# Inputs repacked and transposed, the modulations as fused row sums on VectorE, and the opening stage reordered, in a two-layer Hyena / Mamba-2 backbone

## The reference, cut to what matters

```python
sc, scc = silu(c), silu(c_ctx)                  # vectors of 1024
for i in range(2):
    mod  = (sc  @ ada_w[i] + ada_b[i]).reshape(-1, 1, 9, 1024)   # ada_w[i]: 1024 x 9216
    modc = (scc @ ada_w[i] + ada_b[i]).reshape(1, 1, 9, 1024)
    h  = h  + 0.5 * mod[:, :, 2]  * swiglu(adaln(h,  mod, 0),  ffn_in[i, 0], ffn_out[i, 0])
    hc = hc + 0.5 * modc[:, :, 2] * swiglu(adaln(hc, modc, 0), ffn_in[i, 0], ffn_out[i, 0])
    y, yc = mixer(adaln(h, mod, 3), adaln(hc, modc, 3))
    h = h + mod[:, :, 5] * y                    # hc likewise while it is needed
    ...                                         # second FFN, with mod 6, 7, 8
return rms_norm(h) * final_norm_w
# adaln(x, mod, k) = rms_norm(x) * (1 + mod[k + 1]) + mod[k]
```

## Time and profile before

| what | us |
|---|---|
| runs shown | 2270.53, 2270.56, 2274.07 (median 2270.56) |
| profiled execution, its own time | 2273.82 |
| its span, first to last instruction | 2272.0 |
| PE busy | 2100.8 (92% of the span) |
| DVE busy | 1486.2 (65%) |
| ACT busy | 716.9 (32%) |
| POOL busy | 223.8 (10%) |
| DMA | 292.82 MB, mean 129 GB/s |

### The profile page before, as it was taken

The page is one execution under the profiler, slowest core; times in us unless marked ns, Lnnn a source line. Parts: engine busy times, 40 slices in busy tenths (PEclk is TensorE's granted clock), DMA queues, the critical chain, the costliest instruction groups (busy, mean ns, idle before and its releaser), DMA issues.

```text
span 2272.0 us, 25887 instructions
## 1 busy us (share of the span) xinstructions
PE 2100.8 (92%) x10317; PEld 1736.6 (76%) x10317; DVE 1486.2 (65%) x2027; ACT 716.9 (32%) x920; POOL 223.8 (10%) x172
## 2 busy tenths in 40 slices
PE   5999999999978889999999999999999778888998
PEld 2578888878867768888887888887777764478997
DVE  4576666788965667665777666577775558855544
ACT  2432222232310232222324222222444324444443
POOL 1000000100022410000110000011000005540001
PEclk7999999999998989999999999999999889989999
DMA  7344435544410125442654444354332402334554
GB/s 277 130 131 147 148 105 145 176 130 128 159 66 1 56 93 162 143 139 81 177 162 151 143 146 142 110 163 153 111 112 84 148 25 74 93 111 155 181 167 129
DMA packets 288353, 292.82 MB, mean 129 GB/s; under 512 B 8967, under 2 KB 248496, under 8 KB 286256
## 3 DMA queue, kind: packets, MB, share of 16 engines
q1 hardware_dynamic: 284440, 280.26, 39.1%
q10 hardware_dynamic: 3800, 10.98, 1.2%
HBM read 284.86 MB, written 6.36 MB: 128 GB/s over the span
## 4 chain that ended last, share of the span: by engine, by line
PE 74%; DVE 13%; issue 4%; ACT 3%; DMA 3%; POOL 2%; SPq 0%; ACTq 0%; DVEq 0%; POOLq 0%
PE bank L1564 22%; PE bank L1565 22%; PE bank L1566 22%; DVE wl L912 2%; ACT wh L574 2%; PE bank L1831 2%; DMA raw<-in_ffn_out 1%; DVE avs L930 1%; DVE xl L1002 1%; DVE xt L994 1%; DMA raw<-in_hy_in_w 1%; PE bank L1708 1%; PE bank L1905 1%; POOL mm L1547 1%; PE bank L1624 1%
## 5 line engine op out<-in xcount | busy, mean ns | idle before, releaser
L1564 PE MATMUL bank<-xh,wh 128*128 128x512 f32 (+1 forms) x2120 | 784.4, 370 | 55.0 <-DVE wl L912 28.4
L1565 PE MATMUL bank<-xl,wh 128*128 128x512 f32 (+1 forms) x2120 | 778.6, 367 | 0.0
L1566 PE MATMUL bank<-xh,wl 128*128 128x512 f32 (+1 forms) x2120 | 777.6, 367 | 0.0
L912 DVE TENSOR_TENSOR wl<-raw,wh 128x2048 fp32r<-128x2048 f32 (+1 forms) x196 | 405.1, 2068 | 271.0 <-ACT wh L574 270.6
L574 ACT ACTIVATE wh<-raw 128x2048 fp32r<-128x2048 f32 (+1 forms) x202 | 351.5, 1740 | 578.5 <-PE bank L1566 500.7
L1564 PEld LDWEIGHTS bank<-xh,wh 128*128 128x128 f32 x2120 | 409.5, 193 | 127.2 <-DVE wl L912 31.4
L1566 PEld LDWEIGHTS bank<-xh,wl 128*128 128x128 f32 x2120 | 408.6, 193 | 63.9
L1565 PEld LDWEIGHTS bank<-xl,wh 128*128 128x128 f32 x2120 | 409.4, 193 | 62.2
L1564 PE MATMUL bank<-gh,wh 128*128 128x512 f32 (+1 forms) x704 | 255.6, 363 | 2.4 <-DVE wl L912 1.4
L1566 PE MATMUL bank<-gh,wl 128*128 128x512 f32 (+1 forms) x704 | 255.3, 363 | 0.0
L1565 PE MATMUL bank<-gl,wh 128*128 128x512 f32 (+1 forms) x704 | 255.2, 362 | 0.0
(11 more groups left out here) (225 smaller groups left out, 2019.5 us busy)
## 6 DMA issues: line engine op xcount, KB each, us to landing
raw<-in_ffn_in SPq DMA_DIRECT2D x88, 1024.0 KB, 5.1
raw<-in_ffn_out SPq DMA_DIRECT2D x64, 704.0 KB, 4.7
ada_rawf<-in_ada_w SPq DMA_DIRECT2D x60, 512.0 KB, 4.5
ada_rawo<-in_ada_w SPq DMA_DIRECT2D x48, 512.0 KB, 4.3
raw<-in_mb_in_w SPq DMA_DIRECT2D x24, 1024.0 KB, 5.5
raw<-in_hy_in_w SPq DMA_DIRECT2D x12, 1024.0 KB, 5.2
afb<-decays SPq DMA_DIRECT2D x32, 256.0 KB, 3.2
raw<-in_mb_out_w SPq DMA_DIRECT2D x8, 1024.0 KB, 5.7
```

The costliest lines, as they stand in the source:

```text
L912: dve.tensor_tensor(wl[n_slot][:, 0:cols], raw[r_slot][:, 0:cols], wh[n_slot][:, 0:cols].bitcast(F32), ALU.subtract).then_inc(w_lo, 1)
L1564: pe.matmul(dst, h, x_hi, start=start, stop=False)
L1565: pe.matmul(dst, h, x_lo, start=False, stop=False)
L1566: return pe.matmul(dst, l_, x_hi, start=False, stop=stop)
```

## The change

1. The host hands over `x` and `ctx` already turned (`x_t`, loaded right into `hT`), the small vectors turned (`vec_cols`, into `vecs`), the position network's inputs in one block (`hy_pos`), and `ada_w` turned for all but the first 2048 columns (`ada_rest`: a row is one output column, with its 1024 weights). The output is stored channel-major in eight transfers and turned back on the host.
2. `ada_weigh` now does, for each tile of 128 output columns and each of the two vectors, one operation of 1024 elements that multiplies with `silu(c)` (broadcast over the partitions in `cb0` or `cb1`) and sums the row into `mods` (`accum_out`). A load is two tiles, so four such operations and one small addition of the bias. The constants 1 and 0.5 are put into `vecs` once, or go into the product. `ada_split_hi`, `ada_split_lo`, `ada_sum` and `ada_take` are gone.
3. `silu(c)` goes to device memory once and comes back by `c_load`, ten broadcasts of 512 KB in all: for the `norm`-shared place `cb1` again after each norm, since it lies over `acc` and `rs`.
4. In the opening stage `filters` places its two directions on partitions 0 to 63 and 64 to 127; the norm's squares are made between the units and its sums and spread after the third `spectra`; the transposes are gone; the loads are fewer and in another order; `ada_rows(6)` and `(7)` move past `filters(3)`.

```diff
-            def ada_weigh(n, pieces):
...
-                for kk in range(4):
-                    k = n % 2 * 4 + kk
-                    for c in range(2):
-                        x, w = pieces[kk // 2][:, kk % 2, :], sc[:, k, c:c + 1]
...
-            def ada_split_lo(unit, hi):
...
-            def ada_take(unit, b0, b1, dg):
...
+            def ada_weigh(n, pieces, c_ctx, bases, free=3):
+                if bases:
+                    dve.wait_ge(cb_in, 16 * bases)
+                for i in range(2):
+                    layer, m = ada_place(2 * n + i)
+                    dve.wait_ge(ada_in[i], 16 * (n + 1))
+                    half = 0.5 if m // DT in (2, 8) else 1.0
+                    own(dve.scalar_tensor_tensor(banks[free][:].rearrange("p a n -> p (a n)"), pieces[i][:], half, cb0[:],
+                                                 ALU.mult, ALU.mult, accum_out=mods[layer][:, m, 0:1]))
+                    dve.scalar_tensor_tensor(pieces[i][:], pieces[i][:], half, c_ctx[:], ALU.mult, ALU.mult,
+                                             accum_out=mods[layer][:, m, 1:2]).then_inc(ada_av, 1)
+                layer, m = ada_place(2 * n)
+                dve.wait_ge(ada_av, 2 * n + 2)
+                x = mods[layer][:, m:m + 2, :]
+                own(dve.tensor_tensor(x, x, vecs[:, V_ADA + MODT * layer + m:V_ADA + MODT * layer + m + 2].unsqueeze(2)
+                                      .to_broadcast([P, 2, 2]), ALU.add))
...
-            def ada_sum(unit, b0, b1, hi):
-                pe.wait_ge(ada_lo, unit + 1)
...
-                for c, b in enumerate((b0, b1)):
-                    pe.matmul(b[:], onesr[:], hi[:, c, :], start=True, stop=False)
-                    ins = pe.matmul(b[:], onesr[:], al[:, c, :], start=False, stop=True)
...
             def ada_load(n, pieces):
...
+                for i in range(2):
+                    r = 2 * n + i
+                    if r >= 2:
+                        sp.wait_ge(ada_av, r - 1)
+                    sp.dma_start(pieces[i][:], t["ada_rest"][r * P:r * P + P, :]).then_inc(ada_in[i], 16)
+            def c_load(which, dst):
+                sp.dma_start(dst[:], cscr[which].partition_broadcast(P)).then_inc(cb_in, 16)
...
+                def bases_in():
+                    sp.wait_ge(rms_bc, norms[key].norm + 1)
+                    if key != "10":
+                        c_load(0, cb0)
+                    c_load(1, cb1)
...
             for k in range(DT):
+                if k == 2:
+                    sp.dma_start(hT[:], rows(t["x_t"])).then_inc(s_x, 16)
+                sp.dma_start(ada_k[k][:], t["ada_first"][k * P:k * P + P, :]).then_inc(k_in[k], 16)
```

The opening on ACT:

```diff
                 act.wait_ge(hid_arg, layer + 1)
+                act.activation(hsm[:, 1 if layer == 0 else 4, :], hsm[:, 0, :], ACT.Sin).then_inc(hid_sin, 1)
+                if layer == 0:
+                    act.wait_ge(s_dft, 32)
+                    act.activation(dfh[:], dft[:], ACT.Copy).then_inc(dft_hi, 1)
...
                 if unit:
                     spectra(unit - 1, 2, 5)
+                squares(*((0, 3), (3, 6), (6, 8), (8, 8))[unit])
+            root("00")
```

The opening on PE:

```diff
-                        ins = pe.matmul(bank[2 * d + n][:], hsm[:, 4, n * P:n * P + P], w3[:, c:c + 512],
+                        half = slice(64 * d, 64 * d + 64)
+                        ins = pe.matmul(bank[2 * d + n][:], hsm[half, 4, n * P:n * P + P], w3[half, c:c + 512],
...
             ada_rows(5)
+            ada_rows(6)
             filters(3)
-            ada_rows(6)
+            ada_rows(7)
             spectra(2, 0, 5)
-            ada_rows(7)
...
             spectra(3, 0, 2)
...
+            pe.wait_ge(mods_out, 1)
             pe.wait_ge(s_set, 2)
+            norm_sums("00")
+            spectra(3, 2, 4)
+            norm_spread("00")
+            spectra(3, 4, 5)
```

The end of the kernel on SP:

```diff
-            sp.wait_ge(fin_o, DT)
-            sp.dma_start(out[0].rearrange("(a p) d -> p a d", p=P), ost[:]).then_inc(s_out, 16)
+            for k in range(DT):
+                sp.wait_ge(fin_p, k + 1)
+                sp.dma_start(out[k * P:k * P + P, :], ost[:, k, :]).then_inc(s_out, 16)
```

More of the change, by code:

```diff
@@ L29 @@
 MODT = 9 * DT
[L30 to L32 removed]
+FIRST_M = 2 * DT
 IN_LOADS = 10
@@ L36, with ada_place @@
 XB_LOADS = 4
+C_BASES = {"00": 2, "hy": 4, "01": 6, "10": 8, "mb": 10}
 class Ada:
     def __init__(self, plan, loads):
-        self.load, self.unit = plan["load"], plan["load"] // 2
+        self.load = plan["load"]
         plan["load"] += loads
-def ada_place(unit):
-    u = unit + FIRST_UNIT
-    return u // LAYER_UNITS, u % LAYER_UNITS
+        self.end = plan["load"]
+def ada_place(tile):
+    m = tile + FIRST_M
+    return m // MODT, m % MODT
 V_ADA = 0
@@ L410, in build @@
         fin_p = sem("fin_p")
-        fin_t = sem("fin_t")
-        fin_o = sem("fin_o")
         s_out = sem("s_out")
         rows = lambda a: a.rearrange("(k p) n -> p k n", p=P)
-        ada_v = [rows(t["ada_w"][i]) for i in range(2)]
         ffi_v = [[rows(t["ffn_in"][i, j]) for j in range(2)] for i in range(2)]
@@ L622, in pair @@
                 def pair(i, last):
-                    if ada and i % 2 and i < IN_LOADS:
-                        ada_split_hi(ada_in_ffn[key].unit + i // 2, ah_acc)
                     act.wait_ge(w_used, i * 2 + (pi.w + 1))
@@ L648, in mpair @@
                             u = um * 2 + half
-                            if ada and u == 3:
-                                ada_split_hi(ada_out_ffn[key].unit + i, ah_xh)
                             if not (last and um):
@@ L732, in hy_in_pair @@
                 for u in range(2):
-                    if u and i % 2:
-                        ada_split_hi(ADA_HY.unit + i // 2, ah_acc)
                     if i == 2 and u == 0:
@@ L898, in _ @@
             root("fin", L)
-            for k in range(DT):
-                act.wait_ge(fin_t, k + 1)
-                act.activation(ost[:, :, k * P:k * P + P], bank[k % 4][:, 0:L].rearrange("p (a n) -> p a n", a=2),
-                               ACT.Copy).then_inc(fin_o, 1)
         @block.vector
@@ L1039, in pair @@
                         gate_lo(i - 1)
-                    if ada:
-                        a = ada_in_ffn[key]
-                        if i == 0 and pending is not None:
-                            ada_take(pending, bank[6], bank[4], dg_acc)
-                        if i % 2 == 0 and i:
-                            ada_take(a.unit + i // 2 - 1, bank[6], bank[4], dg_acc)
-                        if i < IN_LOADS:
-                            ada_weigh(a.load + i, ada_rawf)
-                            if i % 2:
-                                ada_split_lo(a.unit + i // 2, ah_acc)
+                    if ada and i < IN_LOADS:
+                        ada_weigh(ada_in_ffn[key].load + i, ada_rawf, cb1, 0 if i else C_BASES[key])
                     if last:
@@ L1160, in _ @@
                         ins.then_inc(p_ready, 1)
-                if unit == 0:
-                    invert_rms(norms["00"], NT)
             for q in (14, 15):
@@ L1166, in _ @@
             open_lo(ffn_in["00"])
+            invert_rms(norms["00"], NT)
+            dve.wait_ge(mods_out, 1)
             ffn("00", 0, 0, True, HYIN)
@@ L1201, in _ @@
                 hy_in_pair(i, i == 5)
-            ada_take(ADA_HY.unit + 2, bank[6], bank[7], dg_acc)
             dve.wait_ge(spec_ld, 16)
@@ L1519, in _ @@
             ffn("00", 2)
-            clear("hy", ADA_HY.unit + HY_LOADS // 2)
+            clear("hy", 2 * ADA_HY.end)
             for x in range(8):
@@ L1534, in _ @@
             ffn("10", 5)
-            clear("mb", ada["load"] // 2)
+            clear("mb", 2 * ADA_XB.end)
             pool.wait_ge(s_set, 1)
@@ L2054 @@
     given.update(_constants())
+    given.update(_layouts(inputs))
     for name, a in given.items():
```

365 lines of the change are left out of this document (125 added, 240 removed).

## The result

The kernel after takes 2205.4 us (median of 4 runs, 2204.8 to 2211.5) against 2270.6 us before (4 runs, 2270.1 to 2274.1): a ratio of 0.9716, 95% interval 0.9696 to 0.9736. 2205 was forecast. A later set of runs of the same kernel gave 2206.7 us (0.9715, 0.9702 to 0.9729). The profiled execution has a span of 2203.2 us, 68.8 less than before.

The account below looks back on a forecast made before the run. TensorE was taken to bound the FFNs, waits for VectorE to cost the projections, and a chain to set the opening. 29.0 + 11.7 + 21 + 3.5 = 65.2 us off 2270.6 gave 2205, own range 2194 to 2214.

Parts of the forecast that it names:

- Ones-matmuls: Mostly in stages where TensorE has no gap: 128 removed matmuls at 0.2262 us each win 29.0 us, 24.5 to 29.
- The fused operation: VectorE's product with row sum in the modulation loads: 1.26 us each, 5.4 us a load where it was 8.1.
- The projections: Hyena and Mamba projection stages: shorter loads shrink TensorE's gaps and slow stretches, 5.7 + 6.0 = 11.7 us, 3 to 14.
- The opening: Up to the first FFN matmul: new order and filter placing win 21 us, from 12 to 28.
- (d): Opening, filters(2) to filters(3): a unit's period of 14.2 us plus an `ada_rows` block of 1.07; filters(3) at 59.8.
- the packing: Opening's filter blocks: two directions on different partition halves run together, each half block costs half; 2 us counted, nothing to 5.
- (b): Opening, filters(0) to filters(1): 26.3 us before; now half a filter block 3.0 and VectorE's operations with rounding 7; start at 26.5.
- (e): Opening, filters(3) to first FFN matmul: 24.7 us before, 29.4 now with the norm's work there; first FFN matmul at 89.2.
- The end: Last products and store: 2.0 us from the removed transposes and 1.5 from eight smaller stores, 3.5 in sum, 1.5 to 5.
- At nothing: Ten broadcasts of `silu(c)` and SP's wait for the norm's spread: costed at nothing; without cover 1 to 4 us at each norm.
- The rivals: Fused sum dear 2219 us (0.17), opening giving 12 2214 (0.13), matmuls giving nothing 2234 (0.03), VectorE the bound 2342 (0.02).
- the fused sum at the scan's rate: Rival on the modulation loads: 2.27 us an operation, 9.5 a load, 2.2 us lost for 11.7 won, 2219 us; chance 0.17.

Follow-up runs that it names:

- experiment 1: Kernel before with ones-matmuls cut to 16 columns: 2262.0 us; kernel after with four full matmuls put back at each old place in the FFNs: 2230.4 us.
- experiment 5: Kernel after with the fused operations in the FFNs' second half made beside each weight block's second chunk, not its first: 2237.2 us.
- Experiment 2: Kernel after with every fused operation made twice: 2280.1 us; with three per tile in place of two, 7.8 us a load: 2230.9 us.
- experiment 3: Kernel after, varied in the opening: no packing 2210.8 us, x first 2213.6, x and norm first 2213.5, sines first 2207.4, sines first with x later 2203.9.

## Why the prediction was right, step by step

**Ones-matmuls, 29.0.** Right in kind: experiment 1 gives back the three layers' whole gain. They are worth 0.19 to 0.21 us each there and not 0.226, so 22.3 us for 24.4 in the FFNs and about 26 for all 128, inside the range of 24.5 to 29.

**The fused operation, 1.26.** 1.225, with 0.08 or 0.14 to read the sum; a load takes 5.2 us for 5.4.

The rule of the Trainium skill ("Vector Engine (DVE) Microarchitecture Reference", "Points that are easy to get wrong"), by which it would be 2.3 us in the prediction's estimate, does not agree with this trace: three groups with 168 of the FFNs' 216 operations have means of 1225 to 1227 ns, all with two fp32 sources in SBUF. The operations of 2.32 us that exist are those beside GpSimd (experiment 5); that they are as long as the estimate is a coincidence.

**The projections, 11.7.** The gaps named held one by one: 3.07 to 0.35 (0.4 forecast), 4.73 to 1.77 (2.1 forecast), 2.51 to 0.63 (1 forecast). Experiment 2 shows the cause. The Hyena stage gave 7.6 to 7.9 where the gaps' 5.7 and twelve matmuls' 2.7 make 8.4: of the 1.5 us counted at the turned tiles only 0.9 came, since the gap ahead grew. Mamba gave more than the sum had: its projection 10.4 (1584.60 to 1739.58 before, 1532.40 to 1676.97 after) for 6.0 and 1.8. Most of that is the slow stretch. I had kept all but 0.7 us of it, but behind the gap of 1.77 the clock stays full, and 10 matmuls more in five microseconds are 2.3 us; with 6.2 of gaps (4.73 to 1.77, 1.72, 1.03 and a first one of 0.54 gone) and 1.8 of matmuls that makes 10.3. And 3.7 us more came behind the projection, where the change touches nothing. Much of that may be the run (463.1 to 468.3, above); part are VectorE's products of the decays, the first of which takes 649 ns for 845 before (31 of each) and the second 679 for 593, so other ones stand beside GpSimd now. That this alignment is the cause was not tested.

**The opening, 21.** 21.9, and the starts were 16.45, 25.55, 41.2, 57.2 and 86.4 for 16.5, 26.5, 44.5, 59.8 and 87 forecast. The last one was right partly by two errors that cancel: `filters(2)` came 3.3 early, as the block that it was to wait for was not late, and the next period was too long: 16.0 us for the 15.3 of (d), from which the packing was to take about 1. With the norm first, where no squares lie between these units, it is 14.2 (55.36 to 69.58), as forecast: half a filter block is 0.85 shorter and the `ada_rows` in the chain 0.85 longer. In the kernel after, VectorE's operations of 0.7 us take up to 1.66 while GpSimd adds squares (the rows below, from the chain), and that is the 1.8 us more.

```profile
43.71 1.54 DVE fel L1072
45.27 1.66 DVE pp L1094
```

Of the parts, the loads' new order is worth about 7 us, the packing 3.3 (2 taken, 0 to 5 given), and the norm's move 0. At (b) I had let the norm and the transposes go together, 16.3 us, and taken back 4.7 for the norm at (e). By experiment 3 the norm has 9.5 of (b), and the end takes back all of it. What is left, 108.36 to 92.94 less the packing, is about 12 us. It is not shown by a run: the transposes of the inputs with their copies, the turned small vectors and the fewer loads were not taken alone. The starts of the version with x and norm first, against those before, say where the 15.4 us with the packing come in: 1.7 at the first block, 7.5 from there to the second, 4.8 to the third, nothing to the fourth, 1.4 behind it. In the 7.5 the chain before goes from the first block by the turning of the small vectors to the first square (31.81), and comes to the norm's sums at 42.97, 19.0 us behind the block's start; now it is 11.5 (22.27 to 33.77). From there to the second block both take 7.3.

**The end, 3.5.** 4.2: from the first product to the span's end it was 10.3 before and is 6.1 after. 2.2 by the transposes (8.1 with one store), 2.0 by the eight stores, 2.0 and 1.5 forecast.

**At nothing.** The broadcasts and SP's wait cost nothing that shows: the gaps behind the norms are the same (2.91 before, 2.91 after at the Hyena norm).

**The sum** was 65.2; 65.2 came in the medians, and 68.8 in the profiled executions, of which the kernel before's was 3.2 above its median. So the nearness of 2205 is in part luck. By the terms, in the profiled pair: ones-matmuls of the FFNs 2.1 less than forecast, Hyena 0.5 less, Mamba 6.3 more (part of it spread), opening 0.9 more, end 0.7 more, and FFN 11 up to the first product 1.8 longer (199.8 to 201.6), which is inside its spread and stood in no term.

**The rivals' prices were wrong, though none came true.** This is the step that failed, and the forecast did not hang on it. I had said that fused operations fit up to 3.4 us each, by one average over the layer. A load of 10.4 us is one with 2.6 us for each operation, and there the kernel is already slower than before. The average hid that the first half has room to spare and the second has 9.7 us in 32, and it left out the projections, which took the other half of the loss. (It also put 8.1 us at all 18 loads, where an `ada_take` stands ahead of every second only. VectorE's busy time in an FFN fell by 34.9 us, and 18 x 2.9 would be 52.) In the same way "the fused sum at the scan's rate" (2.27 us, a load of 9.5) stood at 2219, but 2230.9 was measured at 7.8 already. A straight line from there to the 2280.1 at 10.4 gives 2263, an estimate from above if the FFNs have room for 4.8 us more a load; no run has 9.5. The forecast rested on 1.26 more than its range said: at 7.8 us a load the change would have won 41 and not 65.

## What to carry to other kernels

Read an engine's room in the stretch in which the work is placed, over one period of the loop that places it, not over the stage: VectorE was 60% busy over the layer and 70% in the stretch that gave out, and 5 us more for each load cost 38 us in the three layers and as much in the two projections. A gain at the head of a chain of transfers and engines is worth what is late next allows: 2 us at the first block and 9.5 us at the second were both gone at the end, while 2 MB moved on the queue paid in full (6.7 us at the first block, 7.4 at the end). And where an operation takes longer in one place than in another, look at the other engine at the same moment, but move it only after asking what stands behind it in its own queue.

## What the runs showed of the hardware

- An fp32 operation of VectorE with its inputs in SBUF and an addition of GpSimd do not run side by side. The one that starts second ends 1.10 (VectorE, 1.23 alone) or 1.14 us (GpSimd, 1.28 alone) behind the first, so 1.23 becomes 2.32 us and 1.28 becomes 2.20; the first keeps its length. VectorE's operations with an input in PSUM keep theirs (0.68 us).
- A multiplication of 1024 fp32 elements that also sums its row takes 1.225 us, as the plain reduction does (1.22), and 0.08 us more to read the sum, 0.14 where the product goes to PSUM.
- Matmuls of 16 columns with a full set of weights come every 0.11 us, half the time of 512 columns.
- Two fp32 matmuls of 64 rows each on different halves of the partitions run together: 1.08 us for the 1.93 that they take on the same half.
